# Expert results scattered by GpSimd into token order, with empty places skipped and one weight load held back

## What is computed

```python
def hierarchical_moe(h, ...):            # h: (512, 1024)
    g_idx = top-1 of 4 groups            # g_w: its softmax weight
    top_i = top-2 of the 8 experts in that group, top_w = softmax(top_v)
    combine = onehot(g_idx) * within * g_w
    for g in range(4):                   # 8 experts in each group, 32 in all
        act = silu(h @ w_gate[sl]) * (h @ w_up[sl])      # D_EXPERT = 256
        y  += (act * combine) @ w_down[sl]
x = x + y
```

## Time and profile before

| | us |
|---|---|
| median of 3 runs | 2620.5 (2619.78 to 2621.09) |
| the profiled execution, device time | 2620.24 |
| its span in the trace | 2618.4 |
| TensorE busy in the span | 2420.8 (92%) |
| DVE busy | 1724.7 (66%) |
| ACT busy | 985.4 (38%) |
| GpSimd busy | 405.5 (15%) |
| expert stage, first transpose to last copy | 494 to 761 |

### The profile page before, as it was taken

One profiled execution on the slowest core, in us unless ns is written; L12 is line 12 of the kernel. 1 busy time (PEld: TensorE's weight loads), 2 busy tenths in 40 slices (PEclk: granted clock), 3 DMA queues, 4 the chain that ended last, 5 costly groups with the idle time before them and its releaser, 6 DMA issues.

```text
span 2618.4 us, 31083 instructions
## 1 busy us (share of the span) xinstructions
PE 2420.8 (92%) x12273; PEld 1867.5 (71%) x12273; DVE 1724.7 (66%) x2985; ACT 985.4 (38%) x1265; POOL 405.5 (15%) x299
## 2 busy tenths in 40 slices
PE   6999998688979999999899999989999999999997
PEld 4666775333335445777679999989999878777775
DVE  4635353443216566666527989899996678888986
ACT  4635442121013112774323433345565333333332
POOL 0100000100010000000000011133441334444530
PEclk9999999799989999999999999999999999999998
DMA  5535442799990102111133566789988899999992
GB/s 203 198 147 193 161 161 100 281 425 425 424 379 34 64 0 97 39 59 65 45 117 123 187 233 232 244 285 340 342 340 332 311 335 389 374 379 387 376 372 88
DMA packets 159855, 608.07 MB, mean 232 GB/s; under 512 B 13687, under 2 KB 79415, under 8 KB 126808
## 3 DMA queue, kind: packets, MB, share of 16 engines
q1 hardware_dynamic: 91168, 384.06, 39.1%
q0 software_dynamic: 42480, 154.68, 15.7%
q10 hardware_dynamic: 26056, 67.28, 6.6%
HBM read 535.20 MB, written 70.78 MB: 231 GB/s over the span
## 4 chain that ended last, share of the span: by engine, by line
PE 51%; DVE 22%; DMA 11%; issue 10%; ACT 4%; POOL 1%; ACTq 0%; DVEq 0%; POOLq 0%
DVE window L610 6%; PE P L2762 4%; PE P L2764 4%; PE P L2763 4%; DVE part L610 4%; DMA W<-in_w_up 3%; PE P L2585 3%; PE P L2377 3%; DVE ug L1464 3%; DVE tmp L618 2%; PE P L2173 2%; PE P L2174 2%; PE P L2175 2%; PE P L2438 2%; DMA vg<-in_v,sparse 2%
## 5 line engine op out<-in xcount | busy, mean ns | idle before, releaser
L610 DVE TENSOR_TENSOR part<-raw,part 128x2048 fp32r<-128x2048 f32 x136 | 311.2, 2289 | 169.9 <-ACT part L2026 168.0
L2762 PE MATMUL P<-hr,part 128*128 128x384 f32 (+1 forms) x1136 | 397.7, 350 | 18.7 <-DVE part L610 18.0
L2764 PE MATMUL P<-hr,part 128*128 128x384 f32 (+1 forms) x1136 | 392.2, 345 | 0.0
L2763 PE MATMUL P<-hr,part 128*128 128x384 f32 (+1 forms) x1136 | 391.8, 345 | 0.0
L2881 POOL DMA_INDIRECT ug<-in_ur,sparse x128 | 177.7, 1388 | 1171.7 <-DVE window L1356 707.1
L2866 PE MATMUL P<-part,ge 128*128 128x512 f32 x768 | 302.6, 394 | 12.3 <-DVE part L610 11.6
L2867 PE MATMUL P<-part,ge 128*128 128x512 f32 x768 | 299.6, 390 | 0.0
L2868 PE MATMUL P<-part,ge 128*128 128x512 f32 x768 | 299.5, 390 | 0.0
L2026 ACT ACTIVATE part<-raw 128x2048 fp32r<-128x2048 f32 x136 | 260.5, 1915 | 103.6 <-PE P L2868 80.9
L2762 PEld LDWEIGHTS P<-hr,part 128*128 128x128 f32 x1136 | 214.9, 189 | 30.0 <-DVE part L610 24.0
L2763 PEld LDWEIGHTS P<-hr,part 128*128 128x128 f32 x1136 | 215.0, 189 | 5.1
(11 more groups left out here) (392 smaller groups left out, 4352.2 us busy)
## 6 DMA issues: line engine op xcount, KB each, us to landing
raw<-in_u SPq DMA_DIRECT2D x64, 1024.0 KB
raw<-in_vd SPq DMA_DIRECT2D x64, 1024.0 KB
W<-in_w_up SPq DMA_DIRECT2D x25, 2048.0 KB, 18.0
W<-in_w_in SPq DMA_DIRECT2D x18, 2048.0 KB, 8.9
W<-in_w_down SPq DMA_DIRECT2D x13, 2048.0 KB, 16.1
W<-in_ada_w SPq DMA_DIRECT2D x12, 2048.0 KB, 8.0
a_scratch<-gt ACTq DMA_DIRECT2D x128, 192.0 KB
w_scratch<-window ACTq DMA_DIRECT2D x12, 2048.0 KB, 12.5
```

The costliest lines, as they stand in the source:

```text
L610: return v.tensor_tensor(out=out_, in0=in0, in1=in1, op=op)
L2762: t.matmul(b, wh[:, k, js], HR[0][:, k, lo:S], start=k == 0, stop=False)
L2763: t.matmul(b, wh[:, k, js], HR[1][:, k, lo:S], start=False, stop=False)
L2764: ins = t.matmul(b, wl[:, k, js], HR[0][:, k, lo:S], start=False, stop=k == 7)
```

## The change

1. **Lists.** `TIF` gets 8 columns: token number + 1 for first choices, token number + 1 + 512 for second choices, made early (three small DVE operations behind the router weights' scaling). Bank 6 then holds 0 for an empty place, 1 to 512 for first choices, 513 to 1024 for second. From it DVE makes two lists: `ROW`, the number minus 1, with 4096 added where empty; and `LST`, the same with 512 taken off for second choices. `PU` and its operations go.
2. **Gathers** of `Hd` get a bounds check (`some_rows`): an index over 511 is skipped, without an error. An empty place isn't fetched.
3. **Results** leave by a scatter from GpSimd (`results`): row `ROW[p, i]` of `Yd` gets partition p of `YS`, indices over 1023 are skipped. `Yd` shrinks to 1024 rows: first choices in token order, then second choices. The plain write of ACT and its two waits go.
4. **Reading back** becomes 8 plain DMAs of 512 KB, issued by ACT behind its branch, each of contiguous rows.
5. **The fill** of the extra rows (15 DMAs) goes, with semaphore `zd`.
6. **A load is held**: the first load that goes to slot 5 (the second up weight of tile 1) also waits until the first gather has landed (`gx0` 16). What stands behind it on SP waits with it.

```diff
-        Yd = nc.dram_tensor("y_rows", [128 * NT, D], f32).ap()
+        Yd = nc.dram_tensor("y_rows", [2 * S, D], f32).ap()
...
             rt(tt(WR, WR, par("gf1").unsqueeze(2).broadcast_to([128, 8, 36]), MUL), "wrg")
+            rt(v.tensor_copy(TIF[:, 4:8], TID[:, :]))
+            rt_wait()
+            rt(ts(TIF[:, 0:4], TIF[:, 4:8], 1.0, None, ADD))
+            rt_wait()
+            rt(ts(TIF[:, 4:8], TIF[:, 4:8], 1.0 + S, None, ADD))
...
-            rt(stt(PF[:, 16:24], PF[:, 8:16], 128.0, PF[:, 0:8], MUL, ADD))
-            dve.wait_ge(s["wr"], 32)
-            rt(v.tensor_copy(TIF, TID[:, :]))
-            rt_wait()
-            rt(v.tensor_copy(PU, PF[:, 16:24]), "pu")
...
-            rt(v.tensor_copy(LST, bank[6][:, 0:NT]), "lst")
+            rt(ts(EF2, bank[6][:, 0:NT], 0.5, 4096.0, ALU.is_lt, MUL))
+            rt_wait()
+            rt(ts(EF3, bank[6][:, 0:NT], S + 0.5, -float(S), GT_, MUL))
+            rt(stt(EF2, bank[6][:, 0:NT], -1.0, EF2, ADD, ADD))
+            rt_wait()
+            rt(tt(EF3, EF3, EF2, ADD))
+            rt(v.tensor_copy(ROW, EF2))
+            rt_wait()
+            rt(v.tensor_copy(LST, EF3), "lst")
...
                 a.activation(YS[i % 3][:, 0:512], bank[5], ACT.Copy).then_inc(s["md_a"], 1)
-                act.wait_ge(s["md_a"], i + 1)
-                act.wait_ge(s["md_v"], i + 1)
-                a.dma_start(Yd[i * 128:(i + 1) * 128, :], YS[i % 3]).then_inc(s[f"ys{i % 3}"], 16)
...
+            for i in range(3):
+                act.wait_ge(s[f"ys{i}"], 16 * (6 if i < 1 else 5))
+            act.wait_ge(s["mi_mm"], 2 * NP)
+            act.wait_ge(s["md_mm"], 2 * NP)
+            for q in range(4):
+                for x in range(2):
+                    a.dma_start(GY[q][x], Yd[x * S + q * 128:x * S + q * 128 + 128, :]).then_inc(s[f"gy{q}"], 16)
...
+            def some_rows(dst, src, idx, sem_):
+                return g.indirect_dma_start(out=dst, out_offset=None, in_=src, in_offset=bass.IndirectOffsetOnAxis(ap=idx, axis=0),
+                                            bounds_check=S - 1, oob_is_err=False).then_inc(sem_, 16)
...
-            gp.wait_ge(s["pj_mm"], 12)
-            for i in range(NP, NT):
-                nc.gpsimd.dma_start(Yd[i * 128:(i + 1) * 128, :], CST[:, :]).then_inc(s["zd"], 16)
...
-            for i in range(NP):
-                gp.wait_ge(s["mi_mm"], 2 * (i - 2))
-                rows(GX[i % 3], Hd, LST[:, i:i + 1], s[f"gx{i % 3}"])
+            def results(src, idx, sem_):
+                return g.indirect_dma_start(out=Yd, out_offset=bass.IndirectOffsetOnAxis(ap=idx, axis=0), in_=src, in_offset=None,
+                                            bounds_check=2 * S - 1, oob_is_err=False).then_inc(sem_, 16)
+
+            for i in range(NP + 5):
+                if i < NP:
+                    gp.wait_ge(s["mi_mm"], 2 * (i - 2))
+                    some_rows(GX[i % 3], Hd, LST[:, i:i + 1], s[f"gx{i % 3}"])
+                if i >= 5:
+                    gp.wait_ge(s["md_a"], i - 4)
+                    gp.wait_ge(s["md_v"], i - 4)
+                    results(YS[(i - 5) % 3], ROW[:, i - 5:i - 4], s[f"ys{(i - 5) % 3}"])
...
-            for q in range(4):
-                rows(GY[q][0], Yd, PU[:, q:q + 1], s[f"gy{q}"])
-                rows(GY[q][1], Yd, PU[:, 4 + q:5 + q], s[f"gy{q}"])
...
+            held = next(key for key in slots.order if slots.at[key][0] == 5)
+
             def load(key, pieces):
                 i, _, free = slots.at[key]
                 if free:
                     sp.wait_ge(*free)
+                if key == held:
+                    sp.wait_ge(s["gx0"], 16)
```

More of the change, by code:

```diff
@@ L96, in program @@
         s = {n: sem("s_" + n) for n in (
-            "const par z_v zd x0 x1 x2 x3 nsq nmm nv nw h_v pj_mm pj_a hn_v cv sc_a ada_v ada_mm ada_a att_mm att_a att_v "
+            "const par z_v x0 x1 x2 x3 nsq nmm nv nw h_v pj_mm pj_a hn_v cv sc_a ada_v ada_mm ada_a att_mm att_a att_v "
             "mg_mm mg_v op_mm op_v wr rt_mm rt_v rt_a ht_mm ht_a hd mi_mm mi_a mi_v mu_mm mu_a mu_v mt_mm mm_v md_mm md_a md_v "
@@ L208, in program @@
         AA, SL, TL, IX = (small4(32) for _ in range(4))
-        PF, PU = small(24), kept[:, 8:16].bitcast(u32)
-        LST = kept[:, 16:48].bitcast(u32)[:, 0:NT]
-        TIF = small(4)
+        PF = small(16)
+        LST, ROW = (kept[:, lo:lo + 32].bitcast(u32)[:, 0:NT] for lo in (16, 64))
+        TIF = small(8)
         EI = small(NX_ * 32).rearrange("p (o n) -> p o n", o=NX_)
+        EF2, EF3 = (small(32)[:, 0:NT] for _ in range(2))
         EF, EU = small(16), kept[:, 48:64].bitcast(u32)
@@ L889, in vector_program @@
             rt_wait()
-            rt(tt(OT[:, :, 0:NT].rearrange("p (k q) n -> p k q n", k=2), OT[:, :, 0:NT].rearrange("p (k q) n -> p k q n", k=2),
-                  TIF.unsqueeze(1).unsqueeze(3).broadcast_to([128, 2, 4, NT]), MUL), "lists")
+            rt(tt(OT[:, :, 0:NT], OT[:, :, 0:NT], TIF.unsqueeze(2).broadcast_to([128, 8, NT]), MUL), "lists")
             rt(tt(EI, CUM.unsqueeze(1).broadcast_to([128, NX_, 32]), iota[:, 0:NX_].unsqueeze(2).broadcast_to([128, NX_, 32]), ALU.is_le))
@@ L1846, in scalar_program @@
                     x.wait_ge(s[f"ys{i}"], 16 * (6 if i < 1 else 5))
-                x.wait_ge(s["zd"], 16 * NX_)
                 for j in range(NX_):
-                    i = NP + j
                     x.wait_ge(s["xp"], 6 * j + 1)
@@ L2900, in pool_program @@
                     x.wait_ge(s["xp"], 6 * j)
-                    rows(GX[0], Hd, LST[:, NP + j:NP + 1 + j], s["xg"])
+                    some_rows(GX[0], Hd, LST[:, NP + j:NP + 1 + j], s["xg"])
+                    x.wait_ge(s["xa"], 3 * j + 3)
+                    x.wait_ge(s["xv"], 4 * j + 4)
+                    results(YS[0], ROW[:, NP + j:NP + 1 + j], s["xy"])
                 x.wait_ge(s["xy"], 16 * NX_)
-            for i in range(3):
-                gp.wait_ge(s[f"ys{i}"], 16 * (6 if i < 1 else 5))
-            gp.wait_ge(s["zd"], 16 * NX_)
-            gp.wait_ge(s["mi_mm"], 2 * NP)
-            gp.wait_ge(s["md_mm"], 2 * NP)
-            for q in range(4):
-                rows(GY[q][0], Yd, PU[:, q:q + 1], s[f"gy{q}"])
-                rows(GY[q][1], Yd, PU[:, 4 + q:5 + q], s[f"gy{q}"])
             def row_of_u(k):
```

3 lines of the change are left out of this document (removed).

## The result

| | before | after |
|---|---|---|
| median | 2619.95 us (5 runs, 2619.78 to 2621.09) | 2604.53 us (5 runs, 2603.01 to 2608.64) |
| ratio, 95% interval | | 0.9942 [0.9930, 0.9955] |
| profiled execution / its span | 2620.24 / 2618.4 | 2603.01 / 2601.2 |
| TensorE busy | 2420.8 | 2419.9 |
| DMA traffic, all of the kernel | 608.1 MB | 591.8 MB |

The gain is 15.4 us by medians (17.2 in the two profiled executions), of a forecast 22.2. The traffic falls by 16.3 MB, which is the forecast 7.9 + 4.2 written and 4.2 read. Lines of functions have moved by 8: L2377 is L2385 now, L2438 L2446, L2359 L2367, L2417 L2425, L2501 L2509.

The account below looks back on a forecast made before the run. The expert stage was taken as bound by DMA bytes, with latency at both its ends. Terms 0.6 - 6.0 - 12 - 4.8 = -22.2 took the profiled 2620.2 to 2598 us, forecast range 2591 to 2605 (0.68).

Parts of the forecast that it names:

- Early operations: Three dependent small DVE operations between the router weights' scaling and the `ar` products: +0.6 us, on the path.
- Fill of `y_rows`: Dropping the 7.9 MB fill, during which TensorE is busy and nothing on the path waits for DMA: 0.
- Start: Start of the expert stage: first gather lands at 488.1 instead of 494.06, -6.0 us, bounds +0.5 and -7.5.
- the hold costs 0, however late the gather is: Held loads still land in time, since next loads and tile 0's products hang on the same gather landing: 0.
- Saturated stage: Expert tiles bound by DMA bytes: skipped rows of gathers and results save 12 us, ends 0 and -15.5.
- The bound by TensorE in the tiles with L2425: In four expert tiles TensorE's own work lets through at most 0.9 us instead of 1.23; pitch 16.4 us.
- GpSimd's second DMA: Two DMAs a tile on GpSimd in the expert stage, 2 x 1 us of issue in 17: 0.
- the rival that wanted 8.6 us: Index checks make GpSimd the bound past 8.6 us per DMA: +5 us there, 2671 at 10 us; chance 0.06.
- End: End of the expert stage: last scatter lands sooner, -3.0, plain reads replace gathers, -1.8; together -4.8 us.
- After 800 us: Rest of the kernel, not touched, moves as a block; a change there would have no known reason.
- the no-relief rival: Skips don't relieve the expert stage, which gives 0; most of the start's gain stays: -7.2, 2613 us; chance 0.21.
- The full-relief case: All byte savings arrive, -15.5 in the expert stage and 5.6 at its end: -26.5, 2594 us; 0.05 beyond the range.

Follow-up runs that it names:

- h1: The kernel before with only the hold added: the first load to the H buffer waits for the first gather; median 2614.8 us, ratio 0.9975.
- a1: The kernel after without the hold, the load let go as in the kernel before; median 2611.0 us, ratio 0.9961.
- a3: The kernel after with the three early list operations moved into VectorE's loop over the output projection; median 2604.9 us, ratio 0.9939.
- e1: The kernel after with a fixed pattern for the real lists, odd partitions skipped, 64 of each tile moved; not the layer's result; median 2598.2 us, ratio 0.9911.
- c1: The kernel after with results leaving by ACT's plain writes of all places, gathers still skipped; not the layer's result; median 2610.2 us, ratio 0.9963.
- b3: The kernel after with empty places of results written too, to rows of their own, gathers still skipped; median 2609.2 us, ratio 0.9959.
- a4: The kernel after with VectorE's extra work of tiles 3 to 8 put ahead of its multiplication for the next tile; median 2604.5 us, ratio 0.9933.
- b2: The kernel after with empty places of gathers fetching row 511 instead of being skipped, results still skipped; median 2606.5 us, ratio 0.9952.
- a2: The kernel after with only tile 1's down piece held for the first gather, the up weight ahead going at once; median 2605.6 us, ratio 0.9934.
- d1: The kernel after with the held up weight waiting only for the h_rows writes, the down piece for the first gather; median 2598.5 us, ratio 0.9927.

## Why the prediction was right in sum, and where it was not

At the last up product, hold and skips alone give -1.9 (h1) and -7.2 (a1 against before), together -9.9 (after): they add, with 0.8 of their own. In run time they give about -6 and -10, together -15.4, so they add there too.

1. **Early operations**, +0.6: measured +0.5 on VectorE, right. The clock behind the wait adds 1.0 in the profiled run, with or without them (a3).
2. **Fill of `y_rows`**, 0: without it VectorE's scaling of the router weights starts at 400.82 against 400.66, so nothing was gained by then, right.
3. **Start**, -6.0, of which the list's later end: TensorE started 4.8 us earlier. The gather landed in 3.5, not 4.4; the list came 1.1 us later than forecast (484.76 for 483.05 + 0.6, most of it through the clock ahead), and GpSimd took 0.95 behind it. Right in mechanism and nearly in size. Whether it may be **added** to the rest, two measures answer differently. "-6.0" and "-12" stand in one sum, and so does "the hold costs 0, however late the gather is". At the last up product this is too much: the hold moved the hole from 490..510 to 480..490 and filled little of it, and of 4.6 us 1.9 were left (h1), of 5.2 with the skips 2.7 (a1). But in run time the hold is worth the whole start: means 2615.0 against 2621.1 (h1 and before), 2605.0 against 2611.2 (after and a1). The profiles put the difference behind the last up product, partly in how long one result took to land, partly where no row explains it (the column "rest"). So what is shown is that the gain has shrunk at the stage's end in these executions, not that the time loses it; this stays open.
4. **Saturated stage**, -12 of 15.5, "three quarters": this term was mis-sized. Real lists get 9.9 us at the last up product together with the hold's 1.9, so the skips gave 8.0. With an even load they gave more than the byte sum, which I had called the end of the range: e1 has 18.9 with the hold, 17.0 without. The sum counts only the 11 gathers issued behind 500 us; five more lie ahead of them, but no run puts the 1.5 us down to these. I had named the reason, that the rows left won't lie evenly, and priced it by feel; the fullest engine's share, 37 of 64, was there to be counted and gives an estimate of 9.0. Forecast to the last up product: 0.6 - 6.0 - 12 = -17.4, measured -9.9. The bound by TensorE in the tiles with L2425 was right: forecast pitch 16.4, measured 16.2. Run time says the same of this term: a1 against before is -10 us, where early operations, stage and end were forecast at 0.6 - 12 - 4.8 = -16.2.
5. **GpSimd's second DMA**, 0: checked DMAs take 1.00 us against 0.94 (c1 and b3 agree in the stage), right; the rival that wanted 8.6 us was far off.
6. **End**, -4.8: measured -2.5. Plain reads gave 1.7 (6.76 us from landing to product before, 5.07 after), as forecast 1.8. The scatter landed in 8.85 instead of the forecast 7.2, -1.6, and started 0.75 later behind the copy, through GpSimd. That half of the packets would save half of 6.4 us has no ground in the runs: a scatter of the real list landed in 8.57 to 10.50 (a4 and a1, with after's 8.85 between), one of all rows in 9.77 (b3), and one of 64 rows spread evenly in 10.53 (e1). So part of the 1.6 is chance.
7. **After 800 us** I expected nothing. The profiled run of after gains 4.7 us between its first product with results and its end. The change has no part in it that can be told: with the real lists and the same products there, the other kernels lie between -6.7 (b2) and +2.2 (a2), and a3, which differs from after only in three early operations, has +0.1.

So the total was forecast 2598 and came at 2604.5, inside the range, between the forecast and the no-relief rival (2613), which was wrong in its extreme and right in its reason. That it lies inside the 2591 to 2605 is in part luck: at the first product with results, the last point that the sum speaks of, 12.5 of the 22.2 us are there, and 2620.2 - 12.5 = 2607.7. The other 3 us of the medians lie behind it, where I had expected nothing. The full-relief case needs even lists: e1, 2598.2.

The account itself has a residue. Take 745.8, minus 9.0 for the skips (15.5 for e1), plus the idle time beyond 6.9: h1 744.2 (measured 743.9), after 736.8 (736.0), a1 740.7 (738.6), a2 737.2 (734.6), d1 734.5 (731.0), e1 730.6 (727.0). It misses by up to 3.6 us, always on the late side, and puts a2 behind after, which came ahead of it. So idle time has the right sign for the hold split and the hold alone, but doesn't price them. b3 should cost 8.7 x 37 / 64 = 5.0 and cost 2.2; b2 3.9 and cost 4.2.

## What to carry to other kernels

In a stage that the DMA engines bound, price a saving by the engine that carries most of it, and count rows per engine before taking a mean: skipped rows at the end of each group leave some engines well above the mean (by count 91 of 128 rows stay on the fullest, 64 in the mean). Before you add a gain at the stage's start to a gain in its bytes, look at how much engine idle time the earlier start removes and how much of it is left at the stage's end, here less than 3 of 5 us, and check that against run times, which here gave the whole. Put into the hole what fits (here 2 MB behind the row writes, another 5 us in the trace). Since results now go to rows by token, places inside a tile are free to choose: dealing an expert's tokens over its 64 places instead of filling them from the first should give nearly the even load of e1 with the real lists; it was not tried.

## What the hardware showed

- A place skipped by the bounds check still leaves a packet of under 512 B, 1221 become 3118 in 260 us (2241 in b2 and 2059 in b3, with one direction skipped). At even load they don't slow the weight packets (e1).
- In the seven kernels that skip in both directions with the real lists, the weight packets themselves move slower while they hold an engine, 407 to 417 GB/s against 421 to 423 in the seven others, and the busy share stays at 1.00. So a share of 1.00 at 396 GB/s is not saturation as 1.01 at 424 is; by what mechanism is open.
- A gather of 128 places, half of them skipped, lands in 3.5 us on quiet engines and in 10.8 (median) in the stage, no sooner than a full one before (9.5).
- Behind the same wait, TensorE's granted clock was 0.89 (before), 0.54 (h1, the same queue), 0.50 (after), 0.56 (a3) and 0.79 (b2) from 404 to 408 us; from 0.89 to 0.50 it is 1 us of product time that no instruction explains.
- Behind the first product with results, profiled executions of kernels with the same products there differ by 9 us (-6.7 to +2.2 against before).
